# Down projections with seven products for a pair: the sums of weights moved from the vector engines into transfers that add

## Time and profile before

| | us |
|---|---|
| median of three runs | 2193.94 |
| the profiled execution, by the device | 2195.73 |
| its span in the trace | 2193.9 |
| TensorE busy | 2180.1 (99%) |
| VectorE busy | 1566.5 (71%) |
| ScalarE busy | 1133.5 (52%) |
| GpSimd busy | 711.8 (32%) |
| the load queue of SyncE, share of 16 DMA engines | 55.7% |

### The profile page before, as it was taken

One profiled execution on the slowest core, in us unless ns is written; L12 is line 12 of the kernel. 1 busy time (PEld: TensorE's weight loads), 2 busy tenths in 40 slices (PEclk: granted clock), 3 DMA queues, 4 the chain that ended last, 5 costly groups with the idle time before them and its releaser, 6 DMA issues.

```text
span 2193.9 us, 34076 instructions
## 1 busy us (share of the span) xinstructions
PE 2180.1 (99%) x11511; PEld 1862.4 (85%) x11511; DVE 1566.5 (71%) x2187; ACT 1133.5 (52%) x1720; POOL 711.8 (32%) x625
## 2 busy tenths in 40 slices
PE   9999999999999999999999999999999999999998
PEld 7888988888888888888888887788888888888887
DVE  6876767558657757755878667567778777787775
ACT  6445555545445545454556455465455455554553
POOL 3202320361362263153000033005554355533531
PEclk9999999999999999999999999999999999999999
DMA  7665335556556556566565654545555665555664
GB/s 250 231 224 171 116 130 181 174 184 211 191 182 209 192 184 207 202 194 197 177 199 188 225 171 137 192 163 182 189 195 185 202 198 192 188 191 197 200 207 149
DMA packets 118084, 414.35 MB, mean 189 GB/s; under 512 B 12896, under 2 KB 18048, under 8 KB 117472
## 3 DMA queue, kind: packets, MB, share of 16 engines
q1 hardware_dynamic: 111600, 401.37, 55.7%
q10 hardware_dynamic: 6384, 11.70, 1.7%
HBM read 409.29 MB, written 2.15 MB: 188 GB/s over the span
## 4 chain that ended last, share of the span: by engine, by line
PE 93%; DVE 4%; ACT 1%; DMA 1%; POOL 1%; issue 1%; SPq 0%; DVEq 0%; ACTq 0%; POOLq 0%
PE bank L607 33%; PE bank L615 17%; PE bank L941 6%; PE bank L943 6%; PE bank L942 6%; PE bank L664 2%; PE bank L666 2%; PE bank L665 2%; DVE wboth L1307 2%; PE bank L1269 1%; PE bank L1267 1%; PE bank L1268 1%; PE bank L740 1%; PE bank L1202 1%; PE bank L777 1%; PE bank L917 1%
## 5 line engine op out<-in xcount | busy, mean ns | idle before, releaser
L1307 DVE TENSOR_TENSOR wboth<-raw,wboth 128x1024 fp32r<-128x1024 f32 (+1 forms) x756 | 953.8, 1267 | 468.1 <-ACT wboth L2157 459.8
L2157 ACT CAST wboth<-raw 128x1024 fp32r<-128x1024 f32 (+1 forms) x756 | 773.0, 1034 | 469.3 <-PE bank L943 123.3
L607 PE MATMUL bank<-A,wboth 128*128 128x512 f32 x2928 | 705.4, 392 | 0.5 <-DVE wboth L1307 0.3
L607 PEld LDWEIGHTS bank<-A,wboth 128*128 128x128 f32 x2928 | 536.8, 188 | 105.3 <-issue 1.3
L615 PEld LDWEIGHTS bank<-A,wboth 128*128 128x128 f32 x2928 | 376.7, 191 | 14.8
L615 PE MATMUL bank<-A,wboth 128*128 128x256 f32 x2928 | 384.0, 283 | 0.0
L941 PE MATMUL bank<-wboth,H 128*128 128x512 f32 x508 | 197.8, 389 | 1.2 <-DVE wboth L1307 1.2
L943 PE MATMUL bank<-wboth,H 128*128 128x512 f32 x508 | 197.6, 389 | 0.0
L942 PE MATMUL bank<-wboth,H 128*128 128x512 f32 x508 | 197.6, 389 | 0.0
L2661 POOL TENSOR_TENSOR PT<-z,rs 128x256 f32<-128x256 f32 x88 | 92.5, 1052 | 263.4 <-DVE z L1338 261.3
L2661 POOL TENSOR_TENSOR bias<-z,rs 128x256 f32<-128x256 f32 x64 | 104.7, 1635 | 197.9 <-DVE z L1338 109.4
(11 more groups left out here) (387 smaller groups left out, 3160.7 us busy)
## 6 DMA issues: line engine op xcount, KB each, us to landing
raw<-wstream SPq DMA_DIRECT2D x756, 512.0 KB, 3.4
bias<-bias_rows ACTq DMA_DIRECT2D x6, 512.0 KB, 5.4
x<-xrows ACTq DMA_DIRECT2D x1, 2048.0 KB, 9.1
bias<-grows ACTq DMA_DIRECT2D x2, 1024.0 KB, 6.4
out<-x SPq DMA_DIRECT2D x8, 256.0 KB, 2.1
x<-xT SPq DMA_DIRECT2D x7, 256.0 KB, 5.3
pA<-bias_rows ACTq DMA_DIRECT2D x2, 512.0 KB, 6.9
Sm<-grows ACTq DMA_DIRECT2D x1, 1024.0 KB, 6.6
```

Source lines behind the costliest of these rows:

```text
L607: last = nc.tensor.matmul(bank(j)[:, :], whi[:, s, cols(i)], moving(j, k), start=(k == 0), stop=(k == K - 1))
L1307: V.tensor_tensor(wlo[:, s, 0:w], raw[:, s, 0:w], whi[:, s, 0:w].bitcast(F32), ALU.subtract).then_inc(lo_ready, 1)
L2157: C.copy(whi[:, s, 0:w], raw[:, s, 0:w]).then_inc(hi_ready, 1)
```

## The change

The sums of weights are no longer made by VectorE and ScalarE from `raw`. They are made in device memory, in a new tensor `weight_sums` with two pieces for each group. SyncE copies the pair's two pieces there (`sum_copy`, 1 MB in one transfer, on the queue of the loads, one behind every fourth load of an earlier stage). GpSimd issues transfers that add (`accum_op`): two for each group on other halves of the weights (`sum_first`), then one that adds the first sum to the rest (`sum_last`). They stand between GpSimd's operations of the two attentions, behind them, and for stage `fd2` in chunk 1: a `sum_first` behind each of the first 12 units of `ff1`, and six `sum_last` in `fd1`.

A group now takes four pieces: one whole, one half, and the two pieces of sums, which land in slots of their own (`y` in the first block, `kT` in the second) and go through ScalarE and VectorE as an ordinary split (`sum_hi`, `sum_lo`). A half has 22 pieces instead of 16. The fast pairs are (2, 4, 6) in both halves of all five stages: 6 groups in each, 30 in all. `sides_in` and `copy_side` now stand at `over[0]` = 20 and at piece 44 of 44; `mains_in` at 22 and at 42 and 43. `corners(c, 1)` waits for `sides_in(c, 1)` in all stages. `proj` uses the lower banks first. SyncE's and GpSimd's loops are written out.

```diff
+    def __init__(self, fast):
+        self.fast = fast
+        self.mixed = sorted({m for ms in fast for m in ms})
+        self.groups = [(cp, n, m) for cp, ms in enumerate(fast) for n, m in enumerate(ms)]
+        self.begin, at = {}, 0
+        for cp in range(2):
+            for m in range(8):
+                self.begin[cp, m] = at
+                at += 4 if m in fast[cp] else 2
+        self.middle, self.count = self.begin[1, 0], at
+        self.halves = {self.begin[cp, m] + 1 for cp, _, m in self.groups}
+        self.over = [self.begin[cp, fast[cp][-1]] + 4 for cp in range(2)]
+FIRST = Pairing(((2, 4, 6), (2, 4, 6)))
+SECOND = Pairing(((2, 4, 6), (2, 4, 6)))
-FIRST = Pairing(((3, 5), (3, 5)), sides=12, mains=17, last_sides=28)
-SECOND = Pairing(((4, 6), (2, 4, 6)), sides=14, mains=16, last_sides=32)
...
+    weight_sums = nc.dram_tensor("weight_sums", [2 * NGROUP, P, PW], F32)
...
+            def load_sum(c, i, g, h):
+                slots = 1 if is_down2(c) else 2
+                free = pairing(c).groups[g - slots] if g >= slots else None
+                if free:
+                    sp.wait_ge(lo_ready, PB[stage_at(c)[1]] + pairing(c).begin[free[0], free[2]] + 2 + h + 1)
+                to, landed, _ = sum_slot(c, g, h)
+                sp.dma_start(to, weight_sums[2 * group_of(c, g) + h]).then_inc(landed, 16)
...
+                    if m in at.fast[cp]:
+                        g = at.used(0) * cp + at.fast[cp].index(m)
+                        load(PB[fd] + i, wstream[w + 1], past[0])
+                        load(PB[fd] + i + 1, wstream[w, :, 0:WIDE], past[1])
+                        if g == 0:
+                            sp.wait_ge(sums_done, 16 * group_of(c + 1, 0))
...
+                        for h in range(2):
+                            load_sum(c, i + 2 + h, g, h)
...
+            def sum_copy(c, g):
+                if c and g == 0:
+                    sp.wait_ge(sums_copied, 16 * group_of(c, 0))
+                x, n = first_weight(c, g), group_of(c, g)
+                sp.dma_start(weight_sums[2 * n:2 * n + 2], wstream[x:x + 2]).then_inc(sums_copied, 16)
+            copies_in = {"kv": 0, "q": 1, "ff0": 2, "gate": DN, "q2": DN + 1}
...
+                    arrive(i, 2 * m + 1)
+                    product(main_bank(c, cp, 0), *hidden(2 * m + 1, early), *weights(i, 0))
+                    pe.wait_ge(*mix_ready.at(mix_count(c, at.mixed.index(m) + 1)))
+                    product(main_bank(c, cp, 2), *mix_of(m, 3), *weights(i, 1)).then_inc(piece_used, 1)
                     arrive(i + 1)
+                    product(side_bank(c, cp, ONE), *hidden(2 * m, early), *weights(i + 1, 0), lone, final).then_inc(piece_used, 1)
+                    arrive(i + 2)
+                    product(side_bank(c, cp, FIVE), *mix_of(m, 1), *weights(i + 2, 0), lone, final)
+                    product(side_bank(c, cp, SEVEN), *mix_of(m, 0), *weights(i + 2, 1), lone, final).then_inc(piece_used, 1)
+                    arrive(i + 3)
+                    product(side_bank(c, cp, SIX), *mix_of(m, 2), *weights(i + 3, 1), lone, final).then_inc(t_used.sem, 1)
+                    product(main_bank(c, cp, 1), *hidden(2 * m + 1, late), *weights(i + 3, 0)).then_inc(piece_used, 1)
                 if cp:
                     pe.wait_ge(z_ready, z0 + 4)
...
+                if f < 2:
+                    pe.wait_ge(z_ready, 4 + UB["proj"] - 2 + 2 * f)
+                else:
+                    pe.wait_ge(*banks_taken.at(8 * (FF_CHUNKS - 1)))
+                rows_group(PB["proj"] + f, PB["proj"] + f, UB["proj"] + 2 * f, UB["proj"] + 2 * f, 2, pA, free=True, upper=(f > 1))
...
+                steps_of = {at.over[0]: lambda: sides_in(c, 0), at.middle: lambda: mains_in(c, 0, range(4)),
+                            at.count: lambda: sides_in(c, 1),
+                            at.count - 2: lambda: mains_in(c, 1, range(2)), at.count - 1: lambda: mains_in(c, 1, range(2, 4))}
+                rows_body(o * CHP + PB[fd], PB[fd], at.count, 1, lambda f: None, steps_of, halves=at.halves, c=c)
...
+            def sum_first(c, i):
+                g = i // 2
+                x, n = first_weight(c, g), group_of(c, g)
+                pool.wait_ge(sums_copied, 16 * group_of(c + 1, 0))
+                if i % 2:
+                    pool.dma_start(weight_sums[2 * n + 1, :, 0:WIDE], wstream[x + 1, :, WIDE:], accum_op=ALU.add).then_inc(sums_half, 16)
+                else:
+                    pool.dma_start(weight_sums[2 * n].rearrange("p (f w) -> p f w", f=2), wstream[x:x + 2, :, WIDE:].rearrange("a p w -> p a w"),
+                                   accum_op=ALU.add).then_inc(sums_half, 16)
+            def sum_last(c, g):
+                n = group_of(c, g)
+                pool.wait_ge(sums_half, 32 * group_of(c + 1, 0))
...
+                pool.dma_start(weight_sums[2 * n + 1].rearrange("p (f w) -> p f w", f=2),
+                               weight_sums[2 * n, :, 0:WIDE].unsqueeze(1).to_broadcast([P, 2, WIDE]), accum_op=ALU.add).then_inc(sums_done, 16)
...
+                        if c == 1 and it * 4 + j < 2 * len(FIRST.groups):
+                            sum_first(2, it * 4 + j)
                         if j % 2 and 2 * it + j // 2 in FIRST.mixed and not is_last(c):
                             mix(c, FIRST.mixed.index(2 * it + j // 2), tB, j - 1, j)
...
+                for n in range(len(FIRST.mixed)) if not is_last(c) else ():
                     mix_low(c, n)
+                for g in range(len(FIRST.groups)) if c == 1 else ():
+                    pool.wait_ge(piece_used, SLOTS + PB[fd] + 2 + 2 * g)
+                    sum_last(2, g)
+                for cp in range(2) if not is_last(c) else ():
+                    corners(c, cp)
...
-                if is_down2(c):
-                    pool.wait_ge(*banks_taken.at(c * 8 + (4 + 4 * cp)))
-                else:
-                    _, fd, o = chunk_at(c)
-                    pool.wait_ge(z_ready, o * 24 + (4 + UB[fd] + (8 if cp else 4)))
+                pool.wait_ge(*banks_taken.at(c * 8 + (4 + 4 * cp)))
```

More of the change, by code:

```diff
@@ L63, with used @@
 PW = BLK * P
+class Pairing:
+    def __init__(self, fast):
[10 more added lines that the diff above has]
+        self.over = [self.begin[cp, fast[cp][-1]] + 4 for cp in range(2)]
+    def used(self, cp):
+        return len(self.fast[0]) + (len(self.fast[1]) if cp else 0)
+DN = FF_CHUNKS - 1
+FIRST = Pairing(((2, 4, 6), (2, 4, 6)))
+SECOND = Pairing(((2, 4, 6), (2, 4, 6)))
+PAIRED = {**{f"fd{c}": FIRST for c in range(DN)}, "dn0": SECOND, "dn1": SECOND}
+NGROUP = sum(len(at.groups) for at in PAIRED.values())
+CHP = 64 + 2 * len(FIRST.groups)
 STAGES = [("vs", 2, 16), ("kv", 16, 16), ("cv", 4, 32), ("misc", 3, 2), ("q", 16, 16), ("wo", 8, 16)]
@@ new lines, in sum_copy @@
+            def sum_copy(c, g):
[4 more added lines that the diff above has]
+            copies_in = {"kv": 0, "q": 1, "ff0": 2, "gate": DN, "q2": DN + 1}
+            for name, _, _ in STAGES:
+                count = WB[name]
+                last = min([w for w in WB.values() if w > count], default=NWEIGHT)
+                if name in PAIRED:
+                    load_pairs(DN + int(name[2:]) if name[:2] == "dn" else int(name[2:]))
+                else:
+                    for w in range(count, last):
+                        if PB[name] + w - count >= BLK:
+                            load(PB[name] + w - count, wstream[w])
+                        if name in copies_in and (w - count) % 4 == 3 and (w - count) // 4 < len(pairing(copies_in[name]).groups):
+                            sum_copy(copies_in[name], (w - count) // 4)
@@ L976, in plain @@
-                def plain(i, f):
+                    if cp == 0 and k is not None and is_down2(c):
+                        pe.wait_ge(up_ready, (c - DN) * CH + k + 1)
+                    elif cp == 0 and k is not None:
+                        pe.wait_ge(ff_ready, c * CH + (k + 1))
+                def plain(i, k, f):
                     for t in range(QT):
-                        last = product(main_bank(c, cp, 2 * f + t), *hidden(i, slice(t * P, t * P + P)), *weights(i, f), i == 0, i == 15)
+                        last = product(main_bank(c, cp, 2 * f + t), *hidden(k, slice(t * P, t * P + P)), *weights(i, f), k == 0, k == 15)
@@ L2787, in _ @@
             pool.wait_ge(acc_zero, 1)
+            for g in range(len(SECOND.groups)):
+                pool.wait_ge(piece_used, SLOTS + PB["wo2"] + 16 + 2 * g)
+                sum_last(DN + 1, g)
             pool.wait_ge(rs_ready, 6)
@@ L2826, in _ @@
                 product_lo(n - 1)
-                if n == CH:
-                    pair_sums(DN + c)
+                for m in range(len(SECOND.mixed)) if n == CH else ():
+                    mix_low(DN + c, m)
+                for cp in range(2) if n == CH else ():
+                    corners(DN + c, cp)
                 t0 += n
```

342 lines of the change are left out of this document (147 added, 195 removed).

## The result

The changed kernel takes 2232.82 us (median of four runs, 2229.36 to 2236.22) against 2194.32 for the kernel before: ratio 1.0176, 95% interval 1.0158 to 1.0194. It is slower, as forecast, but by 38.5 us and not by 5.3: outside the range of 2189 to 2213. The profiled execution took 2229.36, its span is 2227.5 (before: 2193.9).

The account below looks back on a forecast made before the run. The prediction took TensorE's order of matmuls to set the time: 7.0 us gained against 12.3 lost, so +5.3 on the 2193.9 us median gives 2199.2 us, slower by 0.24%, with an eight-in-ten range of 2189 to 2213.

Parts of the forecast that it names:

- What hides the transfers themselves: DMA engines in fd0 and q: loads, copies and adding transfers fit or are covered by the lead; cost 0.
- Rival C: Weights come late where adding transfers run, as in fd1: 0 to 15 us of stalls, about 2206; chance 0.15.
- 8 groups more (24 matmuls fewer), stall in fd0: TensorE in the down stages: 5.44 us for fewer matmuls and 1.56 for fd0's stall, together 7.0 us gained.
- handover, five times: Banks passing from cp 0 to cp 1: TensorE stands 0.35 us for the side banks each time, 1.7 in all.
- proj: Third piece of `proj` waits for the side banks: 1.3 us lost, once.
- ring in ff0, ff1, ff2: GpSimd, ScalarE and VectorE's unit cycle makes TensorE late: 0.5 us in ff0, 1.15 each in ff1 and ff2; 2.8.
- first groups, three times: First group of fd0, fd1, fd2, moved to piece 4, waits for `mix_low` and a split: 1.5 us each, 4.5.
- issue of adding transfers in ff1: GpSimd in ff1: issues of 1.0 us hidden in idle time except behind units 5 and 9; 2.0 us lost.
- E: The end of the down stage before; the first take in `ff1` was forecast at 12.36 us behind it.
- A: Edges aren't met: handover and `proj` losses stay, the rest falls to at most 1 us; 2190.4, chance 0.25.
- B: GpSimd's transfer issue costs more than its idle time: at 2.9 us, 15.6 lost instead of 2.0; 2212.8, chance 0.12.
- D: Copies don't spread over the engines or SyncE waits for `sums_done`: tens of microseconds, 2240; chance 0.03.

Follow-up runs that it names:

- e1: The changed kernel without its 90 adding transfers, the copies kept and SyncE waiting for the copies: 2205.36 us, ratio 1.0053.
- g3: The kernel with fast pairs (3, 5, 6) in the first block and adding transfers moved (2213.6 us), with `sides_in(c, 0)` and `copy_side(c, 0)` two steps earlier: 2204.83 us.
- g2: Adding transfers moved, four groups in the first block, early side banks (2192.6 us), then copies in q and q2 later, `sides_in(c, 0)` two steps earlier: 2190.30 us.
- e2: The changed kernel without adding transfers and without copies, sums pieces loaded from the weights themselves: 2204.24 us, ratio 1.0053.
- e5: The changed kernel with adding transfers later in both attentions and fd1's six issued in ff2: 2207.94 us, ratio 1.0061.

## Why the prediction was wrong

**The step that failed** is "What hides the transfers themselves ... I cost all this at nothing". It cost 25.5 us (35.1 less 9.6 over the stages). Its rate was nearly right: forecast share 1.15, measured 1.06 from 170 to 190 us in q and 1.10 from 188 to 196. Two conclusions from it were wrong. First, "the lead covers that" looked at the loads of weights alone. In q and q2 the late transfers are others, small ones of ScalarE's queue, which engines wait for directly and which block the splits behind them. No row of the prediction had them; the page of before lists `bias<-bias_rows` with 5.4 us, and the engines that wait for it stand in the program. Secondly, "about 11 us from its issue to ScalarE's turn" holds for plain pieces. Four pieces of a group last 21 matmuls, 4.8 us, so behind a group the lead is less than half. In fd1, from 683 to 728, the loads' median landing was 8.5 us (4.8 in e1), two of them 12 and 13.6, longer than even the 11 us of plain pieces. Rival C had fd1 right in place and size (0 to 15, measured 12.6), at a chance of 0.15, and didn't know q and q2. That the forecast had the direction right owes nothing to this step: without the adding transfers the kernel is still slower (e1, 2205.4, inside the range), by the order of work alone.

**Point by point**, us:

| step | forecast | measured, by stages of e1 and rows |
|---|---|---|
| 8 groups more (24 matmuls fewer), stall in fd0 | -7.0 | -7.4, if all five stages are taken at g3's and g2's dn0, 82.96; no kernel has fd0 to fd2 with six groups and no stop (g2's fd0 with four: 84.34 for 85.89) |
| handover, five times | 1.7 | 2.1 (0.30 + 0.11 late at the first two matmuls of the second half of dn0; its 83.41 - 82.96 is 0.45) |
| proj | 1.3 | 2.0: a stop of 1.2 as forecast, and one of 1.0 behind the stage |
| ring in ff0, ff1, ff2 | 2.8 | 0.3 + 1.2 + 1.2 |
| first groups, three times | 4.5 | 9.9: 8.1 in the group's stops, the rest in smaller delays at the start of the stage |
| issue of adding transfers in ff1 | 2.0 | 0.4 |
| traffic | 0 | 25.5 (27.5 by the medians, 2232.8 - 2205.4) |

The measured terms add up to 35.2, the stages to 35.1. The first groups are the mis-sized term of the order: the place and both causes were right, but the splits beside mix_low take 2.19 us each, not "1.5 us and more", so that there are stops of 1.3 and 0.7 beside the small one of 0.3 for mix_low. The second stop behind proj is VectorE's and ScalarE's copies out of the banks (`y` L1912), which moved back with the first. The first take in ff1 came at E + 12.37, forecast 12.36.

**Rivals.** A is false: the edges were met everywhere. B is false: an adding transfer of ff1 is shown with 0.8 to 1.1 us, GpSimd's next operation starts 0.58 us behind its start (below), and takes stayed 5.5 us apart. D is false: SyncE has no wait for `sums_done`.

```profile
619.03 0.85 POOL L2740 DMA_DIRECT2D weight_sums<-wstream  x1
619.61 1.32 POOL L2805 TENSOR_TENSOR kT<-Sm 128x256 f32<-128x256 f32 x1
```

**What stays open**: by what rule the other transfers delay ScalarE's. The traces show H at 6.9 us with the loads beside it, 10.3 with the copies too, 13.3 with GpSimd's plain transfers as well and 13.5 with the adding ones in their place, though these take the engines for twice as long. By the Trainium skill, "DMA: Bandwidth & Descriptors", Queues, rings and completion order, each DMA engine takes turns between the queues that have work, packet by packet. That order would make a queue of small packets wait for one packet of each other queue at a time. It fits the step from 10.3 to 13.3, where a queue is added, and the small one to 13.5, since an adding and a plain packet take about the same time each. The number of queues does not explain the step from 6.9 to 10.3, since the copies ride on the queue of the loads. What is special in them is the size: by the pages of e1 and e2 the 30 copies are 480 packets of 64 KB, of an estimated 2.6 us of an engine each (61.9% and 58.4% of 16 engines), where nearly all others have less than 8 KB. No run here tests the rule, or the size of the packets, alone.

## What to carry to other kernels

Before putting traffic into "idle" DMA time, list every transfer that an engine waits for directly, not the main stream alone, and keep new traffic away from those few: here the same 90 transfers cost 27 us at one set of places and 3 at another. Count the lead of a prefetch in time, at the densest stretch of pieces, not in pieces. And put the freeing of a bank ahead of work that depends on a load of the next block.

## What the runs showed of the hardware

- A transfer that adds in device memory takes twice the engines' time of a plain one of the same bytes: 10.3% against 5.1%, by twice the packets (20640, 11040) at about the same time each (0.178, 0.165 us). Those of 512 KB land in 14 us against 7 at these places; in e5, where they run later, the adding ones land in 10.
- GpSimd starts its next operation 0.58 us behind the start of such a transfer's issue, less than the 1 us that I had taken.
- After stops of 3.2 to 3.7 us in q, fd1 and q2 TensorE ran at the lower of its two levels (1.2 GHz; granted clock 0.57 on average from 188 to 196), in fd1 with matmuls 0.43 us apart instead of 0.23 from 724.0 to 727.4. In q the low stretch was longest: 8 us at 0.57 are an estimated 3.4 us lost to the clock, beside the stop of 3.6 itself; the stage grew by 6.6. The rows are those of fd1:

```profile
723.15 0.49 PE L1016 MATMUL bank<-wboth,H 128*128 128x512 f32 x1 [3.72 <-DVE Sm L1863]
...
725.25 0.63 PE L1016 MATMUL bank<-wboth,H 128*128 128x512 f32 x1
725.67 0.63 PE L1017 MATMUL bank<-wboth,H 128*128 128x512 f32 x1
...
727.58 0.40 PE L1016 MATMUL bank<-wboth,H 128*128 128x512 f32 x1
```
